# A mixture-of-experts block on one Trainium2 core: expert rows added to the residual rows in DRAM by accumulating indirect DMAs, and a slot table built from one-hot products

## What is computed

```python
x = x + gate1[:, None, :] * mix
h = modulate(rms_norm(x, norm2_w[l]), shift2, scale2)
ffn = moe_ffn(h, ...)                  # per token: top 4 of 32 experts
x = x + gate2[:, None, :] * ffn
return rms_norm(x, final_norm_w)

# moe_ffn, for one expert and the tokens that chose it
hid = clamped_swiglu(xb @ w_gate_up[e] + b_gate_up[e])
out = hid @ w_down[e] + b_down[e]
y[token] += out * softmax_weight[token, expert]
```

## Time and profile before

| what | value |
|---|---|
| median of three runs | 2203.03 us (2201.9 to 2205.33) |
| the profiled execution | 2187.63 us |
| its span | 2185.8 us, mean granted TensorE clock 0.971 |
| busy PE / DVE / ACT / POOL | 2038.8 / 810.2 / 264.8 / 155.1 us |
| HBM read / written | 537.62 / 25.54 MB |

### The profile page before, as it was taken

One profiled execution on the slowest core, in us unless ns is written; L12 is line 12 of the kernel. 1 busy time (PEld: TensorE's weight loads), 2 busy tenths in 40 slices (PEclk: granted clock), 3 DMA queues, 4 the chain that ended last, 5 costly groups with the idle time before them and its releaser, 6 DMA issues.

```text
span 2185.8 us, 42419 instructions
## 1 busy us (share of the span) xinstructions
PE 2038.8 (93%) x16673; PEld 980.1 (45%) x16673; DVE 810.2 (37%) x1887; ACT 264.8 (12%) x585; POOL 155.1 (7%) x219
## 2 busy tenths in 40 slices
PE   6999999999979999998899999999999999999970
PEld 3564556455644444445343444444444444434430
DVE  1666886687663000043221221221221222222216
ACT  2122112112121000010100100100100100100000
POOL 0011111111110000011200000000000000000002
PEclk9999999999989999996999999999999999999995
DMA  9463333333124222436999999999999999999934
GB/s 316 124 187 119 113 116 93 94 115 96 53 73 144 77 77 67 138 136 240 305 413 404 407 407 402 407 411 405 403 410 403 404 406 406 409 405 403 410 136 179
DMA packets 199129, 563.70 MB, mean 258 GB/s; under 512 B 15181, under 2 KB 135025, under 8 KB 146357
## 3 DMA queue, kind: packets, MB, share of 16 engines
q1 hardware_dynamic: 176431, 528.12, 63.7%
q0 software_dynamic: 6624, 21.77, 2.9%
q10 hardware_dynamic: 16038, 13.32, 1.9%
HBM read 537.62 MB, written 25.54 MB: 258 GB/s over the span
## 4 chain that ended last, share of the span: by engine, by line
PE 48%; DVE 1%; POOL 1%; DMA 1%; issue 0%; ACTq 0%; ACT 0%; POOLq 0%; DVEq 0%
PE ps L1730 30%; PE ps L1752 16%; PE ps L1739 1%; PE ps L1717 1%; POOL ring L616 1%; DVE ring L1400 1%; POOL slot_tok L603 0%; DMA yT<-slot_tok 0%; DMA slot_tok<-tid,slotki 0%; DVE yT L1406 0%; DVE yT L1404 0%; DVE ring L1403 0%; ACTq L851 0%; ACT zs L896 0%; DVE ring L1397 0%
## 5 line engine op out<-in xcount | busy, mean ns | idle before, releaser
L1730 PE MATMUL ps<-ring,hT 128*32 128x512 f32 x6336 | 690.9, 595 | 1.1 <-ACT hT L865 1.1
L1417 PE MATMUL ps<-hT,ring 128*128 128x512 f32 x1008 | 440.4, 595 | 0.0
L1730 PEld LDWEIGHTS ps<-ring,hT 128*32 128x32 f32 x6336 | 203.4, 110 | 461.4 <-issue 457.5
L1752 PE MATMUL ps<-ring,seg 128*32 128x256 f32 x6336 | 348.7, 380 | 3.4 <-ACT seg L874 3.4
L1315 DVE TENSOR_TENSOR hT<-ps,bgu 128x512 f32<-128x512 f32 x99 | 67.9, 686 | 627.2 <-PE ps L1730 627.2
L1417 PEld LDWEIGHTS ps<-hT,ring 128*128 128x128 f32 x1008 | 191.1, 191 | 231.2 <-issue 230.6
L1752 PEld LDWEIGHTS ps<-ring,seg 128*32 128x32 f32 x6336 | 202.5, 110 | 137.5 <-ACT seg L874 3.6
L1018 DVE SCALAR_TENSOR_TENSOR c<-ring,pcur,c 128x512 f32<-128x512 f32 x232 | 155.5, 744 | 0.0
L857 ACT ACTIVATE mm<-hT 128x256 f32<-128x256 f32 x99 | 45.2, 457 | 694.8 <-DVE hT L1317 694.8
L1417 PE MATMUL ps<-yT,ring 128*128 128x512 f32 x256 | 111.2, 592 | 1.0 <-ACT yT L723 1.0
L1417 PE MATMUL ps<-ring,hT 128*128 128x256 f32 x512 | 111.8, 379 | 0.0
(11 more groups left out here) (258 smaller groups left out, 1327.6 us busy)
## 6 DMA issues: line engine op xcount, KB each, us to landing
ring<-in_w_gate_up_dram SPq DMA_DIRECT2D x264, 1024.0 KB, 8.8
ring<-in_w_down_dram SPq DMA_DIRECT2D x132, 1024.0 KB, 7.8
ring<-in_w_ada_dram SPq DMA_DIRECT2D x24, 1024.0 KB, 8.7
ring<-in_w_in_dram SPq DMA_DIRECT2D x48, 512.0 KB, 4.1
ring<-in_w_in_dram SPq DMA_DIRECT2D x16, 1024.0 KB, 5.4
item_rows<-zs ACTq DMA_DIRECT2D x132, 96.0 KB, 5.2
ring<-decay_rows SPq DMA_DIRECT2D x8, 1024.0 KB, 7.2
ring<-in_w_ssm_out_dram SPq DMA_DIRECT2D x8, 1024.0 KB, 5.5
```

The lines of the kernel that those rows point to most:

```text
L1417: last = T.matmul(out_, lhs(k), rhs(k), start=(k == 0), stop=(k == n - 1))
L1730: last = T.matmul(ps[j * GT:(j + 1) * GT, g, :], xT[:, k, g * GT:(g + 1) * GT], gu[:, k, j * GUW:(j + 1) * GUW], start=(k == 0), stop=(k = ...
L1752: last = T.matmul(ps[j * GT:(j + 1) * GT, 3 + g // 2, (g % 2) * DW:(g % 2 + 1) * DW], hidT[:, k % 2, g, k // 2, :], dn[:, k, j * DW:(j + 1 ...
```

## The change

Each expert row is multiplied, on DVE, by its softmax weight and by `gate2` (new tile `g2t`, one quarter of the columns per partition group), still in the tile `orows`. POOL then issues three indirect DMAs per item (`add_rows`), one per group, each of 128 rows of 1 KB, which add the rows to the DRAM tensor `acc_rows`. That tensor starts as the residual rows: SP writes `x2` there while the first weights load. Slots without a token carry an index out of bounds, and their rows are not written. After the last item SP reads `acc_rows` back into `x2`, and only the final norm remains. `item_rows`, `slot_tok`, `rows_out`, the 16 gathers and the 16 scatters are gone.

The slot table is now built on chip. DVE makes for each of the 16 (token tile, choice) pairs a one-hot matrix over the 96 places and, over the 54 items, a one-hot row times the token number and times the weight. PE sums 16 products into a table of 96 by 108 (`all_numbers`), placed after 6 of the 8 chunks of item 0; `spread_numbers` lays this table out by partition, and `slot_rows` makes from it the weights `wslot` and the row indices `sidx`. `token(1)` too now waits for this table.

The parts of the diff that the prediction speaks of ("..." marks cuts):

```diff
+            for t in range(TT):
+                sp.wait_ge(x2_ok, 4 * (t + 1))
+                sp.dma_start(acc_rows[ch(t), :], x2[:, t, :]).then_inc(side_out, 16)
             sp.dma_start(fn, final_norm_w.partition_broadcast(P)).then_inc(fn_in, 16)
 
...
             refill_dn(final, before_final)
-            for t in range(TT):
-                sp.wait_ge(fin_ok, 6 * t + 6)
+            items = sp.value_load(ntot[0:1, 0:1], min_val=NE, max_val=MAXI)
+            plain(nc.sync, orow_out, 16 * NG * items, x_in, 16)
+            for t in range(TT):
+                sp.dma_start(x2[:, t, :], acc_rows[ch(t), :]).then_inc(got_in[t], 16)
+            for t in range(TT):
+                sp.wait_ge(fin_ok, t + 1)
                 sp.dma_start(out_v[:, t, :], x2[:, t, :]).then_inc(out_done, 16)
...
+            def add_rows(i, first=False):
+
+                if first:
+                    pool.wait_ge(side_out, 16 * (1 + TT))
+                else:
+                    pool.wait_ge(orow_out, 16 * NG * i)
+                plain(nc.gpsimd, scaled_ok, 5 * i + 5, const_ok, 15)
+                for g in range(NG):
+                    nc.gpsimd.indirect_dma_start(
+                        acc_quarters, bass.IndirectOffsetOnAxis(ap=scur[:, g:g + 1].bitcast(U32), axis=0),
+                        orows[:, g, :], None, bounds_check=S * NC - 1, oob_is_err=False,
+                        compute_op=ALU.add).then_inc(orow_out, 16)
+
             pool.wait_ge(hrow_out, 16 * TT)
-            pool.wait_ge(side_out, 16 * SIDE)
             gather(0, first=True)
             gather(1)
...
-                nc.gpsimd.indirect_dma_start(
-                    slot_tok, bass.IndirectOffsetOnAxis(ap=slotki[:, s:s + 1].bitcast(U32), axis=0),
-                    tid[:, s // TOPK:s // TOPK + 1], None).then_inc(slot_out, 16)
+            pool.wait_ge(tab_ok, 4)
             items = pool.value_load(ntot[0:1, 0:1], min_val=NE, max_val=MAXI)
-            with pool.Fori(2, items + 1) as i:
+            final = pool.value_load(ntot[0:1, 1:2], min_val=NE - 1, max_val=MAXI - 1)
+            gather(2)
+            add_rows(0, first=True)
+            with pool.Fori(3, items + 1) as i:
                 gather(i)
-            plain(nc.gpsimd, dn_pe, 8 * items, const_ok, 11)
-            for t in range(TT):
-                for k in range(TOPK):
-                    s = t * TOPK + k
-                    nc.gpsimd.indirect_dma_start(
-                        got[:, s, :], None, item_rows,
-                        bass.IndirectOffsetOnAxis(ap=slotki[:, s:s + 1].bitcast(U32), axis=0)).then_inc(got_in[t], 16)
+                add_rows(i - 2)
+            add_rows(final)
             for t in range(TT):
...
-            def rows_out(i):
-                act.wait_ge(orow_ok, 2 * i + 2)
-                for j in range(NC):
-                    act.dma_start(item_rows[bass.ds(i * SLOTS, SLOTS), j * DW:(j + 1) * DW].rearrange("(g t) n -> t g n", g=NG),
-                                  orows[j * GT:(j + 1) * GT, :, :]).then_inc(orow_out, 16)
-
             def tanhs(i):
...
-            rows_out(final)
-            for t in range(TT):
-                act.wait_ge(fin_ok, 6 * t + 5)
+            for t in range(TT):
+                act.wait_ge(got_in[t], 16)
                 if t:
                     act.wait_ge(sq_ok, 2 * TT + t)
                 nc.scalar.activation(orow, x2[:, t, :], ACT.Square, accum_out=ss[:, t:t + 1]).then_inc(sq_ok, 1)
-            plain(nc.scalar, orow_out, 64 * items, x_in, 16)
 
         @block.vector
...
+                    dve.wait_ge(orow_out, 16 * NG * i)
+                V.tensor_copy(wcur[:, :], wslot[:, :, bass.ds(i, 1)].rearrange("p g a -> p (g a)")).then_inc(scaled_ok, 1)
+                V.tensor_copy(scur[:, :], sidx[:, :, bass.ds(i, 1)].rearrange("p g a -> p (g a)")).then_inc(scaled_ok, 1)
                 bias = bdn[:, :].unsqueeze(1)
                 V.scalar_tensor_tensor(orows[:, 0:2, :], ps[:, 3, :].rearrange("p (g n) -> p g n", g=2), 0.5,
                                        bias.to_broadcast([P, 2, DW]), ALU.mult, ALU.add).then_inc(orow_ok, 1)
                 V.scalar_tensor_tensor(orows[:, 2, :], ps[:, 4, 0:DW], 0.5, bdn[:, :], ALU.mult, ALU.add).then_inc(orow_ok, 1)
+                dve.wait_ge(scaled_ok, 5 * i + 1)
+                for g in range(NG):
+                    dve.wait_ge(orow_ok, 2 * i + 1 + g // 2)
+                    V.scalar_tensor_tensor(orows[:, g, :], orows[:, g, :], wcur[:, g:g + 1], g2t, ALU.mult, ALU.mult).then_inc(scaled_ok, 1)
 
             def token(i):
 
...
-            V.tensor_copy(slotki[:, :], slotk[:, :, :].rearrange("p t k -> p (t k)")).then_inc(tab_ok, 1)
+            by_k = [P, TT, TOPK, NE]
+            link(V.tensor_tensor(picked, oh, slot[:, :, :].unsqueeze(2).to_broadcast(by_k), ALU.mult))
+            link(V.tensor_reduce(slotk[:, :, :], picked, AX.X, ALU.add))
...
-                link(V.tensor_scalar(tw[:, t, :], ew[:, t, :], esum[:, t:t + 1], None, ALU.mult))
+            link(V.tensor_tensor(tw[:, :, :], ew[:, :, :], esum[:, :].unsqueeze(2).to_broadcast([P, TT, TOPK]), ALU.mult))
+            in_tab = [P, TOPK, NTAB]
+            for t in range(TT):
+                for k in range(TOPK):
+                    V.tensor_scalar(in_slot[:, t * TOPK + k, :], io96[:, :], placek[:, t, k:k + 1], None, ALU.is_equal).then_inc(asg_ok, 1)
+                here = in_item[:, t, :, 0:NTAB]
+                link(V.tensor_tensor(here, ibase[:, :].unsqueeze(1).to_broadcast(in_tab),
+                                     itemk[:, t, :].unsqueeze(2).to_broadcast(in_tab), ALU.is_equal))
+                link(V.tensor_tensor(in_item[:, t, :, NTAB:], here, tw[:, t, :].unsqueeze(2).to_broadcast(in_tab), ALU.mult))
+                V.tensor_scalar(here, here, tid[:, t:t + 1], None, ALU.mult).then_inc(asg_ok, 1)
+            dve.wait_ge(tok_pe, 2)
+            link(V.tensor_scalar(tok_all, ps[0:SLOTS, 7, 0:NTAB], -1.0, 0.0, ALU.add, ALU.max))
+            token(1)
+            V.tensor_copy(tab_rows, ps[0:SLOTS, 7, 0:2 * NTAB]).then_inc(asg_ok, 1)
+            V.memset(rel[0:1, 0:1], 0.0)
...
-                n = 6 * t
-                dve.wait_ge(got_in[t], 16 * TOPK)
-                acc = got[:, t * TOPK, :]
-                V.tensor_scalar(acc, acc, tw[:, t, 0:1], None, ALU.mult).then_inc(fin_ok, 1)
-                for k in range(1, TOPK):
-                    dve.wait_ge(fin_ok, n + k)
-                    V.scalar_tensor_tensor(acc, got[:, t * TOPK + k, :], tw[:, t, k:k + 1], acc, ALU.mult,
-                                           ALU.add).then_inc(fin_ok, 1)
-                dve.wait_ge(fin_ok, n + 4)
-                link(V.tensor_tensor(acc, acc, g2row, ALU.mult))
-                V.tensor_tensor(x2[:, t, :], x2[:, t, :], acc, ALU.add).then_inc(fin_ok, 1)
...
+            def first_numbers():
+
+                pe.wait_ge(sel_ok, 5)
                 acc_k(ps[0:SLOTS, 7, 500:501], lambda t: sel[:, t, :], lambda t: tid[:, t:t + 1], TT).then_inc(tok_pe, 1)
+
+            def all_numbers():
+
+                n = TT * TOPK
+                for a in range(n):
+                    t, k = a // TOPK, a % TOPK
+                    pe.wait_ge(asg_ok, 5 * (t + 1))
+                    last = T.matmul(ps[0:SLOTS, 7, 0:2 * NTAB], in_slot[:, a, :], in_item[:, t, k, :], start=(a == 0), stop=(a == n - 1))
+                last.then_inc(tok_pe, 1)
+
+            def spread_numbers():
+
+                pe.wait_ge(asg_ok, 5 * TT + 1)
+                for g in range(NG):
+                    for j in range(NC):
+                        last = T.matmul(ps[j * GT:(j + 1) * GT, 7, g * 2 * NTAB:(g + 1) * 2 * NTAB],
+                                        ident[0:SLOTS, g * GT:(g + 1) * GT], tab_rows, start=True, stop=True)
+                last.then_inc(tok_pe, 1)
 
             def tokens_in(i, first=False):
                 pe.wait_ge(xg_in, 16 * (i + 1))
...
             def item(i, first=False):
-                gate_up(i, range(4))
-                if first:
-                    pe.wait_ge(slot_in, 16)
-                    pe.wait_ge(tok_ok, 2)
-                    T.transpose(ps[0:SLOTS, 7, 0:MAXI + 1], tok_rows, ident[0:MAXI + 1, 0:MAXI + 1]).then_inc(tok_pe, 1)
-                gate_up(i, range(4, KT))
...
             tokens_in(0, first=True)
-            gate_up(0, range(4), first=True)
-            numbers(1)
-            gate_up(0, range(4, KT))
+            gate_up(0, range(6), first=True)
+            all_numbers()
+            gate_up(0, range(6, KT))
             tokens_in(1, first=True)
+            spread_numbers()
             hidden(0)
-            pe.wait_ge(tab_ok, 5)
```

More of the change, by code:

```diff
@@ L135, in build @@
         wo = ring[:, 16384:].rearrange("p (k n) -> p k n", k=KT)
-        got = ring[:, 0:16 * 1024].rearrange("p (s n) -> p s n", s=16)
         hT = sb("hT", [P, KT, S])
@@ L414, in follow_rest @@
                 load_arow(g + 1)
```

(54 more changed lines are left out.)

82 lines of the change are left out of this document (37 added, 45 removed).

## The result

The changed kernel takes 2174.1 us (median, 2171.8 to 2178.5) against 2202.8 for the kernel before: a ratio of 0.9873, 95% interval 0.9858 to 0.9888. That is 28.7 us less; 41 were forecast. On another chip it was 2175.1 against 2195.9, 0.9904 (0.9883 to 0.9924), or 20.8 us less.

A forecast was written before the change was run, and what follows sets the result against it. PE was taken to set the pace, at 32.96 us per item. Savings of 2.5 us at `hidden` and 38.6 at the end, less 0.1 where the experts start, made 41.0: 2203.0 to 2162 us, range 2150 to 2195.

The forecast's parts named there:

- The likeliest case: Whole kernel: the forecast of 2162 us holds, with 2150 to 2170 as its own range; chance 0.66.
- the slower case: End and items: a slower end gives 2170 us, with small stalls per item up to 2190; chance 0.16.
- All three signs: Expert items: PE idle for the gather in every item, weights landing above 8.8 us and growing, an add over 8.6 us.
- The forecast for the profiled execution: Whole kernel: 41.0 us off the profiled 2187.63 us, giving 2146.6 us.
- The end: After PE's last product: the span ends 25.8 us behind it instead of 64.4, saving 38.6 us.
- `hidden`: Last item: ACT copies hidden values without issuing row writes first, so the copy starts 2.5 us earlier.
- Where the experts start: Items 0 and 1: 3.2 us more small products and 0.3 over the pause, less 3.4 of table wait: 0.1 us lost.
- The steady part: Every item: the gather behind the adds still has 2.1 to 5.6 us to spare, so it costs nothing.
- The rival's price: Every item: adds of 10.4 us make the gather late, PE waits 3.1 us per item, 2258 us; chance 0.10.
- The engines: Steady items: weights landing in 8.8 of 30.4 us show room for adds; rival of full engines, 2252 us, chance 0.04.
- The sum: Whole kernel: 2.5 + 38.6 - 0.1 = 41.0 us saved, from 2203.0 to 2162 us.
- its slower end: After the last product: three adds one after another at 5.2 us, the last landing 8.3 us later, giving 2170 us.

The follow-up runs named there:

- plain writes: The changed kernel with the three indirect DMAs overwriting the accumulator rows instead of adding, summation left out: 2149.7 us.
- the early gather: The changed kernel with POOL gathering for item i+3 ahead of the adds of item i, token numbers written two items ahead: 2147.6 us.
- the adds twice: The changed kernel with the gather one turn earlier and each add repeated into a DRAM tensor that nothing reads: 2215.8 us.
- empty adds: The changed kernel with the bound of the three adds at 0, so that nearly every row is out of bounds and no data moves: 2147.5 us.

## Why the prediction was right, and where it was not

The sign and the range held, 2150 to 2195 for 2174. The likeliest case, 2150 to 2170, did not come true: it missed by 4 us, and 12 us of the 41 did not come. What came was the slower case with "a stall of a fraction of a us per item". All three signs that it had named for being wrong showed: PE idle before the transposes with the gather as releaser, weights landing later than in 8.8 us, and an add over 8.6 us. The forecast for the profiled execution, 2146.6, missed by 25 us (2171.8). By the table of stretches the change is worth 21.2 us without its first row, by the medians 28.7 on one chip and 20.8 on the other. What the 28.7 has over the other two figures no trace explains; that it brings the result nearer to the forecast is luck as far as the runs show.

*The end.* Right to a tenth, T + 25.75 against T + 25.8 (T is the end of the last product), but by luck in its parts, which cancel. POOL's third issue starts at T + 7.2, not 5.6, since an add occupies POOL for 1.55 us, not 0.97, and POOL begins 0.4 us later. SP reads only 2.8 us behind it, so the adds land faster here than the 5.2 taken; the reads go out at T + 9.95 against 11.1. From there to the last tile's final norm it took 11.5 us against 9.0: ACT had to wait for the third tile, where the prediction had ACT decide and not the reads, and 0.8 us more lay between the last square and its norm.

```profile
2161.60 1.06 ACT L899 ACTIVATE zs<-yT 128x1024 f32<-128x1024 f32 x1 [1.68 <-DMA yT<-acc_rows]
```

And from the norm to the end it took 4.3 us, not 5.6.

*`hidden`.* 2.35 us against 2.5; alone it gives 2 to 8.

*Where the experts start.* 3.20 us for the small products against 4.0, 0.76 against 1.3 for the spreading ones, and the pause before `hidden` hides them as said. `hidden` begins 1.2 us later than before, counted from the first gate and up product (31.35 against 30.14), where the prediction had 3.5; the 3.4 us of the old table's wait left as said, so the two traces differ by 2.1 us of gain. The balance also rested on one sample of a wait that varies. Alone, the table gives 4 to 9 us.

*The steady part.* This is the step that failed, a term put at nothing: "The last of them is issued at 1518.8, and lands by 1524.0 with the median of the earlier trace rows ... Still 2.1 us to spare, so I cost it at nothing." It cost 0.71 us per item, 21.9 us (26 in the trace from the other chip). The mechanism was the one named, a gather in one queue behind the adds; what was off was the size. An add takes 9.7 us to land, nearly twice the 5.2, and past the 8.6 at which the prediction had a late gather eat the whole gain. By the prediction the gather goes out 7.3 us behind the down products, lands in 8.8 and has 5.6 to spare. It goes out at 9.1, which is POOL's longer issue (3 by 0.58 = 1.75 us), and lands in 13.2, 4.4 later; behind plain writes it landed in 9.1, so 4.1 of these 4.4 are the accumulating. The rival's price was too high: at 9.7 us it would have made PE wait over 2 us. Adds and gather overlap in part: the gather has landed 15.0 us behind the last add's issue (1.84 + 13.2), not 9.7 + 8.8 = 18.5.

The rule of the Trainium skill, "DMA: Bandwidth & Descriptors", section "Queues, rings and completion order", that an engine works a ring off in order (the page says it of SP's and ACT's queues, this one is POOL's), fits the 13.2 us behind adds against 8.8 us with the gather issued ahead of them. With that of the Trainium skill, "Collectives: The Full Stack", section "Part 3: Why 7× under link rate", that an add reads two sources and so runs at half the rate, the traces agree: 5.3% against 2.6% of the engines' time for the same bytes. The prediction had named it as speaking for the doubling and then took the plain write's median all the same.

*The engines.* The prediction read 8.8 us of landing in 30.4 us allowed as room. It is no such measure. 1.2 us of row writes per item went and 1.8 us of adds came (5.3% of 950 us, over 28 items); this moved the landing from 8.8 to 15.6 us, with 17 to 20 us once the gather's wait was gone. Another 1.6 us (13.6 less 9.1% of 34.8, where 9.1% is the early gather's share) brought waits. The DMA engines' total share doesn't show it either: it reads 1.02 before, 1.03 after and 1.03 with the adds twice.

*The sum.* The parts come from two chips on which the kernel before takes 2195.9 us: 6.6 for the table and 4.8 for `hidden` (ratios times 2196, from the one), 38.7 for the end by the traces, less 26.4 for the gather (from the other): 23.7 us. Measured on the latter: 20.8, interval 17 to 26. Small slips of the prediction decided nothing: it starts the third add at 1518.8 by one reckoning and, by the gather's 1520.5, near 1519.2 by the other, and the 8.3 us of its slower end are 7.9 by its own terms (3.1 + 3 by 5.2, less 10.8).

## What to carry to other kernels

Work put ahead of a DMA whose landing an engine soon needs, in the same queue, is paid for by that DMA, even when its own result is needed by nobody for a long time: put the gather first, or issue it a turn earlier, and check its slack against the landing time of the new work, not of the nearest known one. Price an accumulating indirect DMA at half again the issue and twice the engine time of a plain one, as measured here with rows of 1 KB. A prefetch that lands early does not show how much more the engines can take: here the landing time nearly doubled for 0.6 us more of engine time per item, before any wait for weights showed, and 1.6 us more cost 1.8 us per item. Reckon with the engine time that the new work adds, and test it by doubling the work.

## What the runs showed of the hardware

- An accumulating indirect DMA of 128 rows of 1 KB occupies POOL for 1.55 us, a plain one for 0.98. Rows out of bounds save none of the issue, and empty adds still take 1.0% of engine time (4.6% less the 3.6% of the gathers).
- The same pause of PE, 3.3 to 3.4 us ahead of the last down products, left them at 10.57 us in two executions of the kernel before (granted clock 1.00) and went with 13.28 us in one with the table alone, where the clock was 0.66 from 2110 to 2120 us (0.50, its lower level, from 2111 to 2117):

```profile
2112.30 13.28 PE L1754 MATMUL ps<-ring,seg 128*32 128x256 f32 x192 [3.38 <-ACT seg L873]
```

After a pause of 1.04 us the granted clock stayed at 1.00 in all eleven traces, too few to show that the shorter pause removes the risk. And one of these, with the plain writes, needed 12.13 us at that clock, for which no cause is shown.
